# The end of an attention: earlier tiles' logits and probabilities beside the last tile's second output half, and squares by halves

## The reference, cut to what matters

```python
xl = xl + gt_a * out_lat                        # residual after the output projection
hl = modulate(xl, g_ffn[l], sh_f, sc_f)         # rmsnorm(x) * g * (1 + scale) + shift
# expert_choice_ffn:
logits = jnp.einsum('bnd,de->ben', h, w_router)
affinity = jax.nn.softmax(logits, axis=1)       # over the 16 experts
gates, idx = lax.top_k(affinity, cap)           # each expert takes cap = n / 8 tokens
xs = h[idx]                                     # then w_gate, w_up, w_down of every expert
```

## Time and profile before

| | us |
|---|---|
| median of 3 runs | 2153.51 |
| lowest, highest | 2150.78, 2155.71 |
| span of the profiled execution | 2157.7 |
| TensorE busy in it | 1970.7 (91%) |
| VectorE busy | 676.9 (31%) |
| ScalarE busy | 529.7 (25%) |
| mean granted clock of TensorE | 0.971 |

### The profile page before, as it was taken

How to read it: one execution, slowest core, us unless ns; L and a number is a source line. 1 busy time by engine, 2 the same in 40 slices (tenths; PEclk the granted TensorE clock), 3 DMA queues, 4 the chain that set the end, 5 groups by cost and what they waited for, 6 DMA issues and landing times. The chain is left out here.

```text
span 2157.7 us, 27259 instructions
## 1 busy us (share of the span) xinstructions
PE 1970.7 (91%) x10878; PEld 931.5 (43%) x10878; DVE 676.9 (31%) x1753; ACT 529.7 (25%) x1220; POOL 156.9 (7%) x155
## 2 busy tenths in 40 slices
PE   5999989999979999999999899889996898887875
PEld 2436465555633332323323556465554333333322
DVE  3322345666650100101001632366666011110203
ACT  3211154565531000100100321166553010000001
POOL 1100010000010010020100201100000000000000
PEclk8999979999989999999999999999998899999998
DMA  9742020000189999999999302110008899999995
GB/s 352 287 161 81 0 79 1 1 2 1 40 322 414 425 365 418 380 391 419 363 414 420 137 20 78 23 57 1 1 1 342 361 427 426 427 426 427 427 427 213
DMA packets 90935, 515.66 MB, mean 239 GB/s; under 512 B 10594, under 2 KB 15628, under 8 KB 36540
## 3 DMA queue, kind: packets, MB, share of 16 engines
q1 hardware_dynamic: 84496, 493.29, 56.4%
q0 software_dynamic: 4416, 15.21, 2.4%
q10 hardware_dynamic: 1900, 5.43, 0.6%
HBM read 498.69 MB, written 15.20 MB: 238 GB/s over the span
## 5 line engine op out<-in xcount | busy, mean ns | idle before, releaser
L712 PE MATMUL psS<-arena 128*64 128x512 f32 (+9 forms) x4552 | 1136.0, 556 | 70.8 <-DMA arena<-in_w_up 23.1
L712 PEld LDWEIGHTS psS<-arena 128*64 128x64 f32 (+4 forms) x4552 | 450.0, 158 | 666.2 <-issue 585.1
L715 PE MATMUL psT<-ident,arena 128*128 128x128 f32 (+1 forms) x1036 | 171.6, 289 | 47.3 <-DVE arena L2053 13.2
L1930 DVE TENSOR_REDUCE mx<-psS 128x1 f32<-128x768 f32 (+2 forms) x200 | 165.5, 827 | 152.1 <-PE psS L712 150.4
L1281 ACT ACTIVATE arena<-psT 128x768 f32<-128x768 f32 (+7 forms) x261 | 150.3, 577 | 244.0 <-PE psT L715 230.3
L1281 ACT ACTIVATE arena<-psS 128x128 f32<-128x128 f32 (+5 forms) x158 | 61.8, 421 | 572.1 <-PE psS L712 527.9
L2106 DVE TENSOR_TENSOR arena<-arena,psS 128x512 f32<-128x512 f32 x32 | 20.5, 684 | 549.6 <-PE psS L712 549.6
L715 PEld LDWEIGHTS psT<-ident,arena 128*128 128x128 f32 (+1 forms) x1036 | 119.5, 144 | 147.3 <-issue 107.9
L712 PE MATMUL psT<-arena 128*32 128x512 f32 x1536 | 174.5, 595 | 0.0
L1281 ACT ACTIVATE arena<-psS,nb 128x768 f32<-128x768 f32 (+2 forms) x200 | 158.1, 794 | 1.4
L712 PE MATMUL psM<-arena 128*128 128x512 f32 x288 | 140.1, 608 | 0.0
(11 more groups left out here) (223 smaller groups left out, 1285.5 us busy)
## 6 DMA issues: line engine op xcount, KB each, us to landing
arena<-in_w_gate SPq DMA_DIRECT2D x117, 1024.0 KB, 12.7
arena<-in_w_up SPq DMA_DIRECT2D x116, 1024.0 KB, 18.2
arena<-in_w_down SPq DMA_DIRECT2D x116, 1024.0 KB, 17.7
arena<-in_w_mod SPq DMA_DIRECT2D x48, 1024.0 KB, 7.4
arena<-in_w_in SPq DMA_DIRECT2D x6, 2048.0 KB, 7.8
arena<-in_w_out SPq DMA_DIRECT2D x8, 512.0 KB, 7.7
arena<-in_w_out SPq DMA_DIRECT2D x2, 2048.0 KB, 15.1
normed_rows<-arena ACTq DMA_DIRECT2D x8, 512.0 KB, 8.1
```

The lines of the kernel that those rows point to most:

```text
L712: return nc.tensor.matmul(o, lhsT, rhs, start=start, stop=stop)
L715: return nc.tensor.transpose(o, in_, ident[0:n, 0:n])
L1930: link(V.reduce_max(mx[:, par:par + 1], view(S, 0, P, 0, (512, 2), (1, n)), axis=AX.XY))
```

## The change

The order of the tail is rewritten on three engines; no other part of the kernel is touched.

TensorE runs the early logits between the two output halves, and cuts the second half in pieces: three of its eight matmuls, `by_token`, two matmuls, the first half of the last tile's transposes, three matmuls. The other four transposes, the second half of the last logits and the last affinities follow. ScalarE takes the last tile's squares in two instructions of 512 columns with a sum each, the first of them and the exponents of `probabilities(0)` ahead of the turned rows. VectorE computes the half sum's share of the root and `probabilities(0)` ahead of the second half's product, copies the earlier affinities ahead of the turned rows, and then puts the two sums together.

```diff
-                output_half(n_tiles - 1, 0)
-                output_half(n_tiles - 1, 1)
+                output_half(n_tiles - 1, 0, 0, KD)
                 early_logits(4, lat_tiles)
-                turn_rows(n_tiles - 1, 0)
-                turn_rows(n_tiles - 1, 1)
+                output_half(n_tiles - 1, 1, 0, 3)
                 if ctx_tiles:
                     by_token(ctx_tiles)
                 by_token(lat_tiles).then_inc(z["lp"], 1)
+                output_half(n_tiles - 1, 1, 3, 5)
+                turn_rows(n_tiles - 1, 0)
+                output_half(n_tiles - 1, 1, 5, KD)
                 last_logits(0)
-                last_logits(1)
                 pe.wait_ge(z["prb"], 2 * l + 1)
                 affinities(tl[:-1])
+                turn_rows(n_tiles - 1, 1)
+                last_logits(1)
...
+                def squares_half(h):
+
+                    i = len(tiles) - 1
+                    t = tiles[i]
+                    act.wait_ge(z["oe"], 2 * halves_through(l, i, h))
+                    if h == 0:
+                        act.wait_ge(z["fxn_sq"], l * TT + i)
+                    else:
+                        act.wait_ge(z["half_sq"], l + 1)
+                    a_(ar[:, PB + h * 512:PB + h * 512 + 512], X[:, t * D + h * 512:t * D + h * 512 + 512], ACT.Square,
+                       accum_out=ss[:, 14 + h:15 + h]).then_inc(z["fxn_sq" if h else "half_sq"], 1)
...
+                squares_half(0)
+                exponents(0)
                 turned_rows(len(tl) - 1)
-                squares(len(tl) - 1)
-                exponents(0)
+                squares_half(1)
...
+                def last_root_half():
+
+                    dve.wait_ge(z["half_sq"], l + 1)
+                    link(V.tensor_scalar(rn[:, 6:7], ss[:, 14:15], 1.0 / D, EPS, ALU.mult, ALU.add))
+
+                def last_root_begin():
+
+                    dve.wait_ge(z["fxn_sq"], l * TT + len(tiles))
+                    link(V.scalar_tensor_tensor(pw[:, 0:1], ss[:, 15:16], 1.0 / D, rn[:, 6:7], ALU.mult, ALU.add))
+                    powers[0] += 1
+                    dve.sem_inc(s_pin, 1)
```

More of the change, by code:

```diff
@@ L403, in backbone_program @@
                      "P O mj me gp ge ce") for l in range(L)]
-        once = {n: sem(n) for n in "open want gd gt gtev rbp rb fg fgev yh yl wb wo lgev pe_ex prb at dup dupT ffn_done xready fxn_sq fxn xr lp st xt xtd lgp lgpc xp done silu prod hp Cn bn qs S T oj oe nb PTa rr Oc Cf he y win0 win1 mixed Og xg cp".split()}
+        once = {n: sem(n) for n in "half_sq open want gd gt gtev rbp rb fg fgev yh yl wb wo lgev pe_ex prb at dup dupT ffn_done xready fxn_sq fxn xr lp st xt xtd lgp lgpc xp done silu prod hp Cn bn qs S T oj oe nb PTa rr Oc Cf he y win0 win1 mixed Og xg cp".split()}
         for z in Z:
@@ L847, in output_piece, with output_half @@
                         last.then_inc(z["oj"], 1)
-                def output_half(i, h):
-                    if h == 0:
+                def output_half(i, h, k0, k1):
+                    if h == 0 and k0 == 0:
                         output_ready(i)
                         pe.wait_ge(z["oe"], 2 * halves_through(l, i, 0) - 2)
-                    for k in range(KD):
+                    for k in range(k0, k1):
                         q, w = QN + tiles[i] * QNW + k * P, WOUT + k * D + h * 512
                         last = mm(bank(7 - h), ar[:, q:q + P], ar[:, w:w + 512], k == 0, k == KD - 1)
-                    last.then_inc(z["oj"], 1)
+                    if k1 == KD:
+                        last.then_inc(z["oj"], 1)
                 def scores(s):
@@ L2029, in _ @@
                 root_end(0, last)
-                for h in range(2):
-                    output_product(last, h, 7 - h)
-                    output_sum(last, h, 7 - h)
+                output_product(last, 0, 7)
+                output_sum(last, 0, 7)
                 dve.wait_ge(z["lgp"], l + 1)
                 V.tensor_copy(ar[:, LGT + CTX:LGT + CTX + (TL - 1) * P], bank(4, w=(TL - 1) * P)).then_inc(z["lgpc"], 1)
+                last_root_half()
+                probabilities(0)
+                output_product(last, 1, 6)
+                output_sum(last, 1, 6)
+                affinities(0)
                 turned_rows(last)
-                root_begin(last, 1)
-                probabilities(0)
+                last_root_begin()
                 root_end(last, 1)
-                affinities(0)
                 probabilities(1)
```

## The result

The first measurement gave 2162.62 us as the median of 4 runs (2159.34 to 2165.51) against 2152.15 for 4 runs of the kernel before: ratio 1.0040, with an interval of 1.0023 to 1.0058. Timed again with 12 runs against 35, it was 2159.74 against 2155.41: ratio 1.0023, 1.0014 to 1.0031, which on 2155 us is +5.0 us (the ratios are those on record; the plain quotients of the medians are 1.0049 and 1.0020). The change makes the kernel slower by both.

What follows compares the result with a forecast made beforehand. The chain through the end of the attention to the gather bounds the kernel, not weight transfers. Layer 0 +3.8, layer 1 +1.5, gather -0.2 make +5.1, applied to the median 2153.51: 2158.6 us (+0.24%), range 2154.5 to 2161.5.

Steps and rivals of the forecast that it cites:

- H comes later: TensorE: H, the end of output half 1's last matmul, comes 2.8 us later in layer 1, at 611.4 in layer 0.
- VectorE held by ScalarE in layer 0: Half 0's squares wait behind five row stores, so VectorE's product of half 1 starts 2.4 us after its matmuls.
- From the product to the power: Half 1's product through sum, transposes and copy: the root's power is asked for at 616.9 (layer 0) and 1649.45 (layer 1).
- D: Rival: TensorE's half clock holds through transposes, last logits and experts' first matmuls in both layers; +8 us, 2161.5; chance 0.08.
- From the power to the marker: Power's round trip 2.05, exponent 1.52 after the store's start; marker (selection's first MAX8) +3.8 in layer 0, +1.5 in layer 1.
- The gather: Layer 1's gather of chosen rows, 1.5 us later, meets less of the DMA queue: gain 0 to 0.7, 0.2 taken.
- A delay passes to the end: A delay before the gather of chosen rows reaches the kernel's end undiminished, once in each layer.
- A: Rival: neither in-order wait on ScalarE binds; +1.4 less 0.2, not slower by the bound, 2154.7 us; chance 0.17 with its halves.
- C: Rival: small groups slide into TensorE's wide weight loads, H hardly moves, no wait binds; -4.7, 2148.8 us; chance 0.06.
- B: Rival: the delay is swallowed, a weight transfer sets the experts' start or end; 0 to +1, 2154 us; chance 0.07.

Runs made afterwards that it cites:

- squares_early: Changed kernel with ScalarE's half 0 squares ahead of the third row store and earlier tiles' exponents ahead of the fourth; +1.7 us against the kernel before.
- after: The whole change against the kernel before, timed and profiled twice: ratio 1.0040 first, 1.0023 (+5.0 us) again.
- only_layer0: Kernel before with the change made in layer 0 alone, layer 1 in the old order; +4.1 us against the kernel before.
- only_layer1: Kernel before with the change made in layer 1 alone, layer 0 in the old order; +2.6 us against the kernel before.
- the short tail: Kernel before with squares by halves, ScalarE and VectorE reordered around them, last affinities in another PSUM bank, TensorE's order kept; ratio 0.9981, again 0.9984.
- all_three: Changed kernel with half 0's squares ahead of the third store and last exponents ahead of the last store; +1.9 us against the kernel before.
- exponents_first: Changed kernel with the last tile's exponents ahead of its row store on ScalarE; +3.0 us against the kernel before.

## Why the prediction was right, point by point

- **Direction and size.** Forecast +5.1, which lies in both measured intervals (5.0 to 12.5 and 3.0 to 6.7); the second, better measurement has +5.0, and its median of 2159.74 lies in the range of 2154.5 to 2161.5. The first median, 2162.62, lies 1.1 above the range. The forecast applied the shift to a median of 2153.51 of three runs; the larger sets of runs of the kernel before since then have medians of 2154.8 to 2155.9, so a part of that is the base.
- **H comes later.** Forecast 2.8 in layer 1, measured 9.63 - 6.87 = 2.76. In layer 0 forecast 3.3, measured 3.2 where nothing hides it (squares_early). The early logits alone were 1.6, 0.2 above their length of 1.43.
- **VectorE held by ScalarE in layer 0.** Forecast product at 613.75, 11.55 behind the product of half 0; measured 11.50. The half square took 0.73 with its read (607.92 to 608.65), for 0.7 taken.
- **From the product to the power.** In layer 1 forecast 2.85 (1646.6 to 1649.45), measured 3.00. In layer 0 forecast 3.15, measured 4.09, 3.19 and 3.80 (after, after_again, only_layer0). Here a term was missing from the sum, the half clock. The last logits' wait of 2.2 for the turned rows, moved behind the exponents, wasn't in it either, but it is in all three profiles, and the one with 3.19 shows that by itself it costs next to nothing. In that one the clock stays full up to 615, and the five affinity transposes take 0.71:

```profile
612.00:614.00 2.00, 0.75 (x7) 0.75 (x7) 1.50 (x6) 0.75 (x2) 0.00 (x0) 1.00 1.02 416
614.00:616.00 2.00, 1.78 (x12) 1.07 (x11) 1.76 (x5) 0.72 (x2) 0.00 (x0) 0.83 0.14 55
```

In the other two they take 1.23 and the four of the rows 1.06, at 0.50. I had the clock as a rival of its own (D) at 0.5 for each group of four transposes; in layer 0 it came true in two executions of three and cost 0.6 to 0.9 there, far from D's whole +8. Why the clock falls in some executions and not in others, after the same idle time, no run shows.
- **From the power to the marker.** The power's round trip was 1.95 and 1.96, 0.1 less than the 2.05 taken. The exponent starts 1.55 and 1.58 behind the store, forecast 1.52. Together these make the markers +3.9 (mean) and +1.6, forecast +3.8 and +1.5. That layer 0 agrees to 0.1 is in part luck: the sum put the marker 20.5 behind the product of half 0 and the three profiles have 20.95 in the mean, for want of the half clock in the sum; but the kernel before has 17.00 in the mean and not the 16.73 of the profile that I worked from, and the two errors nearly cancel.
- **The gather.** I took 0.2 from a gather that meets less of the queue. In layer 1 the first gather took 4.4 to land in both profiles of the changed kernel, against 5.2 and 5.0 before, but TensorE then waited for the second one (the 5.25 in the chain above). In only_layer1, whose gather starts as late, the first took 5.1, so the shorter landing isn't a sure effect of the later start. In the five profiles with the marker at 18.4 the experts' first matmuls come 45.8 to 46.1 behind layer 1's product of half 0, in the three with 16.79 it is 44.4 to 44.7: +1.4 on average where the marker has +1.6. So 0.2 fits what passed on, and no run shows that it comes from the gather. In the other direction more is lost: in the two profiles of the short tail the gather starts 1.7 earlier and takes 6.0 and 5.9 to land, and the experts' first matmuls come only 0.9 and 1.1 earlier. The line is that of the changed kernel's first gather, at 1673 to 1675, answering to the earlier trace rows:

```profile
DMA to landing us min/median/max: 4.4/4.4/4.4
```

- **A delay passes to the end.** No interval in the table excludes the markers' sum, but most are wide. The fourteen profiles together say more. From layer 0's product of half 0 to layer 1's are 1031.6 to 1038.8 us, and this time grows by 0.96 us (standard error 0.19) for each us by which layer 0's marker is later. From layer 1's product to the end of the span are 517.1 to 521.1, and this grows by 0.88 (0.20) for each us of layer 1's marker. So what the tails lose or win reaches the end in the main; that a tenth or two of it is lost on the way can't be told.
- **The rivals.** A (no wait binds) is the kernel all_three, forecast +1.2 after the gather, measured +1.9. Its way from the start of half 1's product to the marker was forecast at 8.2 and 7.9 and is 8.9 and 8.0; layer 0's excess has the size of the wait that is left there. C failed on TensorE's part: nothing slides into the wide stream. B was not seen.

## What to carry to other kernels

Work beside a wait is cheaper than the same work ahead of what is waited for: the small matmuls ahead of the end of the last wide ones delay it by 1.6 us, a little more than their length, and only 0.8 to 0.9 of that comes back behind it. When a step is put ahead in one engine's queue, ask what its operand stands behind in the queue of the engine that makes it; here five stores on ScalarE turned a prepaid step on VectorE into a wait of 2.3 us. And where a shortcut shortens the way to an instruction, look at what stands ahead of it in its queue: a store that was harmless became the bound.

## What the runs showed that I had not expected

Executions of one kernel differ by more than this change is worth (2152.3 to 2158.9 for the kernel before in one set of 35), and the profiles show one place: the attention of layer 0, far from the edit, in how long TensorE's granted clock is at the half level. The stretch table has this for 300 to 400 us of the kernel before:

```profile
300.00:400.00 100.00, 92.10 (x611) 53.21 (x612) 57.53 (x177) 54.29 (x158) 8.29 (x14) 0.95 0.00 1
```

of its second profile:

```profile
300.00:400.00 100.00, 91.37 (x627) 52.59 (x628) 58.97 (x174) 54.20 (x155) 8.58 (x15) 0.98 0.00 1
```

and of exponents_first:

```profile
300.00:400.00 100.00, 92.37 (x607) 53.67 (x608) 56.13 (x173) 52.82 (x155) 8.27 (x14) 0.93 0.00 1
```

With granted clocks of 0.95, 0.98 and 0.93 the product of half 0 in layer 0 starts at 602.20, 598.10 and 603.12, although all three run the same instructions up to there. Other stretches add to it, but a marker counted from a point ahead of the edit is free of all of them; in layer 1, where it repeats within 0.03, it told an effect of 0.4 us that 12 runs against 35 didn't.
